# One layer of a hybrid decoder: the four output tiles in one piece, the router's work behind them

## What is computed

```python
y = jax.nn.sigmoid(gate_a) * y_a + jax.nn.sigmoid(gate_b) * y_b      # attention and LRU branch
x = _layer_norm(ALPHA * x + gate1 * (y @ w_out[l]), ln1_g[l], ln1_b[l])
u = x * (1.0 + scale2) + shift2
f = _grouped_moe(u, router_w, router_b, moe_w_gate[l], moe_w_up[l], moe_w_down[l])
x = _layer_norm(ALPHA * x + gate2 * f, ln2_g[l], ln2_b[l])
```

## Time and profile before

| what | value |
|---|---|
| runs | 768.04, 767.47, 769.25 us |
| median | 768.04 us |
| profiled execution | 767.53 us, span in the trace 765.4 us |
| TensorE matmul busy | 647.1 us (85% of the span) |
| VectorE busy | 344.2 us (45%) |
| ScalarE busy | 250.9 us (33%) |
| mean granted TensorE clock | 0.939 |
| DMA | 189.78 MB, 248 GB/s in the mean |

### The profile page before, as it was taken

The page is one execution under the profiler, slowest core; times in us unless marked ns, Lnnn a source line. Parts: engine busy times, 40 slices in busy tenths (PEclk is TensorE's granted clock), DMA queues, the critical chain, the costliest instruction groups (busy, mean ns, idle before and its releaser), DMA issues.

```text
span 765.4 us, 15490 instructions
## 1 busy us (share of the span) xinstructions
PE 647.1 (85%) x5985; PEld 424.4 (55%) x5986; DVE 344.2 (45%) x657; ACT 250.9 (33%) x522; POOL 98.2 (13%) x185
## 2 busy tenths in 40 slices
PE   0799999998989799999999339899999999999700
PEld 0275666676767577777787224455555545555400
DVE  0265444478888775585675653111111101111058
ACT  0234434557444564465401201111111111111144
POOL 0131000200000000000000032122222212222140
PEclk9999999999999899999999559999999999999955
DMA  9999767292311322213881998999999999961162
GB/s 298 373 313 308 249 220 238 105 314 79 111 44 41 99 66 82 83 56 111 296 363 74 393 419 316 421 418 418 420 419 419 418 419 420 418 261 41 48 219 110
DMA packets 83874, 189.78 MB, mean 248 GB/s; under 512 B 7384, under 2 KB 59832, under 8 KB 68480
## 3 DMA queue, kind: packets, MB, share of 16 engines
q1 hardware_dynamic: 67616, 149.05, 51.7%
q0 software_dynamic: 7376, 32.26, 11.9%
q10 hardware_dynamic: 8848, 8.01, 3.2%
HBM read 175.23 MB, written 14.07 MB: 247 GB/s over the span
## 4 chain that ended last, share of the span: by engine, by line
PE 63%; DMA 12%; DVE 12%; ACT 6%; issue 4%; SPq 2%; ACTq 0%; POOL 0%; POOLq 0%; DVEq 0%
PE psum L1485 17%; PE psum L1496 9%; DMA raw<-in_w_in_dram 7%; PE psum L1293 6%; PE psum L1295 6%; PE psum L1294 6%; DMA wu<-in_moe_w_up_dram 3%; PE psum L1414 2%; PE psum L1416 2%; PE psum L1415 2%; PE psum L1468 2%; PE psum L1259 2%; PE psum L1475 2%; SPq L398 1%; PE psum L1336 1%
## 5 line engine op out<-in xcount | busy, mean ns | idle before, releaser
L1485 PE MATMUL psum<-wg,xs 128*32 128x256 f32 x1280 | 149.8, 386 | 3.8 <-issue 2.1
L1485 PE MATMUL psum<-wu,xs 128*32 128x256 f32 x1280 | 149.2, 386 | 0.0
L1293 PE MATMUL psum<-uh,whi 128*128 128x512 f32 x336 | 137.9, 410 | 1.7 <-DVE wlo L875 1.7
L1295 PE MATMUL psum<-uh,wlo 128*128 128x512 f32 x336 | 131.3, 391 | 0.0
L1294 PE MATMUL psum<-ul,whi 128*128 128x512 f32 x336 | 131.3, 391 | 0.0
L1485 PEld LDWEIGHTS psum<-wg,xs 128*32 128x32 f32 x1280 | 73.0, 111 | 57.1 <-issue 5.5
L1192 DVE TENSOR_TENSOR h_sb<-psum,hsil 64x256 f32<-64x256 f32 x40 | 17.1, 427 | 151.8 <-ACT hsil L784 151.8
L875 DVE TENSOR_TENSOR wlo<-raw,whi 128x1024 fp32r<-128x1024 f32 x42 | 51.4, 1224 | 68.7 <-ACT whi L611 68.5
L1496 PE MATMUL psum<-wd,hT 128*32 128x256 f32 x1280 | 77.4, 382 | 0.4 <-DVE hT L1196 0.4
L1293 PEld LDWEIGHTS psum<-uh,whi 128*128 128x128 f32 x336 | 63.3, 189 | 23.4 <-issue 7.4
L1485 PEld LDWEIGHTS psum<-wu,xs 128*32 128x32 f32 x1280 | 72.0, 111 | 0.0
(11 more groups left out here) (258 smaller groups left out, 842.7 us busy)
## 6 DMA issues: line engine op xcount, KB each, us to landing
wg<-in_moe_w_gate_dram SPq DMA_DIRECT2D x32, 1024.0 KB
wu<-in_moe_w_up_dram SPq DMA_DIRECT2D x32, 1024.0 KB
wd<-in_moe_w_down_dram SPq DMA_DIRECT2D x32, 1024.0 KB
raw<-in_w_in_dram SPq DMA_DIRECT2D x42, 512.0 KB, 3.9
ada<-in_ada_w_dram POOLq DMA_DIRECT2D x16, 1024.0 KB, 5.2
ada<-in_ada_w_dram SPq DMA_DIRECT2D x8, 1024.0 KB, 17.1
y_d<-ysb ACTq DMA_DIRECT2D x160, 32.0 KB
y_d<-zrow POOLq DMA_DIRECT2D x8, 512.0 KB, 6.4
```

What stands on the lines that cost most here:

```text
L1293: mmul(bank[s % 2], h[:, k, :], uh[:, k, :], start=(k == 0), stop=False)
L1295: ins = mmul(bank[s % 2], l[:, k, :], uh[:, k, :], start=False, stop=(k == KT - 1))
L1485: ins = mmul(psum[32 * g:32 * g + 32, 0, 0:256], xs[:, k % 2, k // 2, :], wgu[slot][g // 2][:, k, (g % 2) * 256:(g % 2) * 256 + 256], star ...
```

## The change

TensorE issues the four output tiles one after the other, and only then the router's work of all four tiles. u2 gets four buffers instead of two, and VectorE's waits for the two-buffer scheme go. ScalarE's stream gets the matching order: the square roots and stores of tiles 0 to 2 first, then the copies, with the square root of tile 3 behind the copies of tile 1. SP reads the rows a2 and b2 right behind gate1, with waits for projections 40 and 41, and ahead of the x tiles. No arithmetic is changed.

```diff
-        u2 = [at(R_W + 4 * KB * i, f"u2_{i}", [P, D])[0] for i in range(2)]
+        u2 = [at(R_W + KB * o_, f"u2_{i}", [P, D])[0] for i, o_ in enumerate((0, 4, 28, 32))]
...
             sp.wait_ge(S["proj_ps"], NPROJ - 2)
             sp.dma_start(gate1r[:, :], row_of(0)).then_inc(rows_in, 16)
+            sp.dma_start(a2r[:, :], row_of(3)).then_inc(rows_in, 16)
+            sp.wait_ge(S["proj_ps"], NPROJ - 1)
+            sp.dma_start(b2r[:, :], row_of(1)).then_inc(rows_in, 16)
             sp.wait_ge(S["proj_ps"], NPROJ)
             for t in range(NT):
                 sp.dma_start(x1[:, t, :], x[0, t * P:(t + 1) * P, :]).then_inc(x1_in, 16)
-                if t == 0:
-                    sp.dma_start(a2r[:, :], row_of(3)).then_inc(rows_in, 16)
-                    sp.dma_start(b2r[:, :], row_of(1)).then_inc(rows_in, 16)
...
-            ln_sqrt(0)
-            store_u2(0)
-            ln_sqrt(1)
+            for t in range(NT - 1):
+                ln_sqrt(t)
+                store_u2(t)
             u2_columns(0)
-            store_u2(1)
             logit_parts(0)
             u2_columns(1)
-            ln_sqrt(2)
-            store_u2(2)
+            ln_sqrt(NT - 1)
             logit_parts(1)
             u2_columns(2)
-            ln_sqrt(3)
             logit_parts(2)
-            store_u2(3)
-            u2_columns(3)
-            logit_parts(3)
+            store_u2(NT - 1)
+            u2_columns(NT - 1)
+            logit_parts(NT - 1)
...
-                if t >= 2:
-                    dve.wait_ge(S["u2T_ps"], 2 * (t - 1))
-                    dve.wait_ge(u2_st[t % 2], 16 * (t // 2))
-                V.scalar_tensor_tensor(u2[t % 2][:, :].rearrange("t (k p) -> t p k", k=KT), by_k(zt), rstd[:, t:t + 1],
+                V.scalar_tensor_tensor(u2[t][:, :].rearrange("t (k p) -> t p k", k=KT), by_k(zt), rstd[:, t:t + 1],
...
-            out_tile(0)
-            out_tile(1)
-            to_router(0)
-            out_tile(2)
-            logit_parts(0)
-            to_router(1)
-            logits(0)
-            out_tile(3)
-            logit_parts(1)
-            to_router(2)
-            logits(1)
-            logit_parts(2)
-            to_router(3)
-            logits(2)
-            logit_parts(3)
-            logits(3)
+            for t in range(NT):
+                out_tile(t)
+            for t in range(NT):
+                to_router(t)
+                if t >= 1:
+                    logits(t - 1)
+                logit_parts(t)
+            logits(NT - 1)
```

More of the change, by code:

```diff
@@ L740, in store_u2 @@
                 act.wait_ge(S["u2_done"], t + 1)
-                act.dma_start(u2_d[t * P:(t + 1) * P, :], u2[t % 2][:, :]).then_inc(u2_st[t % 2], 16)
+                act.dma_start(u2_d[t * P:(t + 1) * P, :], u2[t][:, :]).then_inc(u2_st[t % 2], 16)
             def u2_columns(t):
@@ L1384, in to_router @@
                         ins = nc.tensor.transpose(psum[:, 4 + half, (k % 4) * P:(k % 4 + 1) * P],
-                                                  u2[t % 2][:, k * P:(k + 1) * P], ident)
+                                                  u2[t][:, k * P:(k + 1) * P], ident)
                     ins.then_inc(S["u2T_ps"], 1)
```

## The result

The changed kernel takes **763.65 us** in the median of 6 runs (761.84 to 764.76), the kernel before beside it 767.82 (767.37 to 769.25, 6 runs). The ratio is 0.9941, 95% interval 0.9925 to 0.9957: 3.3 to 5.8 us faster, against 5.2 to 5.4 forecast, and inside the range. The profiled execution is one of 764.76 us, the slowest of the six; its span is 762.9 (765.4 before).

A forecast was written before the change was run, and what follows sets the result against it. It took TensorE's products, VectorE's tile 3 normalisation, then TensorE's tail as the bounding chain before routing. 3.1 us from products plus 2.3 from the tail gave 5.4: 762.1 for the profiled execution, 762.6 median, range 761.0 to 767.2.

The forecast's parts named there:

- Products in one piece: TensorE's output products: interleaved router work moves behind tile 3's products, which then end 3.1 us earlier.
- VectorE and the buffers: VectorE's normalisation: same instructions; the two removed waits cost nothing before but would cost now without four buffers.
- The cover of three tiles: Router work of tiles 0 to 2, 6.9 us, hides under tile 3's 7.6 us normalisation with 0.7 to spare: cost nothing.
- ScalarE and SP: ScalarE's new order (tile 3's square root, bounds 0 to 0.3 us) and SP's earlier row reads: both taken as nothing.
- The tail: Tile 3's transposes to routing: 3.3 us at the upper clock against 5.63, 2.3 us gained; bounds 0 and 2.3.
- case A: The main forecast: products' 3.1 us and the tail's 2.3 us both gained, 762.6 us; chance 0.48.
- B: Clock lost at tile 3, around 422 to 424 us: only the products' 3.1 us stay, 764.9 us; chance 0.18.
- Behind it, nothing: Routing, gather and expert loop shift whole; the gather stays 6.2 us, so no gain or loss is added there.
- C: Clock lost inside the router block, at 418.9 us: gain of 1.2 us, 766.8 us; chance 0.15.
- E: Clock lost as soon as the products end: routing 0.7 us later, 768.7 us, or 770.3 at worst; chance 0.06.
- D: Gather ends with the third expert's weight stream, so its end moves by only 3.1 us: 764.9 us; chance 0.07.

The follow-up runs named there:

- e4: Kernel before with four u2 buffers and without VectorE's two waits, old order kept: 767.76 us, ratio 1.0006.
- e3: Changed kernel's order on all engines, but u2 in two buffers with VectorE's two waits: 767.22 us, ratio 0.9998 to the kernel before.
- e9: Changed kernel with the transposes of tiles 0 to 2 issued twice: 763.97 us, ratio 0.9955 to the kernel before.
- e10: Kernel before with only the early reads of rows a2 and b2 added: 768.02 us, ratio 1.0001.
- e12: Kernel before with five filler matmuls in TensorE's idle time ahead of tile 3's transposes, run again for its trace: 766.28 us, ratio 0.9981.
- e1: Changed kernel once more, without an edit: 763.96 us over 12 runs, ratio 0.9959 to the kernel before.
- e5: Changed kernel with one filler matmul of constants in the gap before tile 3's transposes: 763.97 us, ratio 0.9954 to the kernel before.
- e2: Changed kernel with the a2 and b2 row reads put back behind the first x tile: 761.94 us, ratio 0.9942 to the kernel before.
- e6: Changed kernel with eight unread transposes of tile 0's u2 as filler before tile 3's transposes: 762.60 us, ratio 0.9929 to the kernel before.
- e7: Changed kernel with four filler matmuls before the expert loop's first transposes: 762.97 us, ratio 0.9934 to the kernel before.
- e11: Changed kernel with row reads put back, one filler before tile 3's transposes and four before the expert loop: 762.48 us, ratio 0.9935 to the kernel before.

## Why the prediction was right, point by point

*Products in one piece, 3.1 us.* Right, 3.26 in each of the traces with the new order and four buffers. The 0.15 above the forecast 3.11 is the slower start of products after each change of work, which I left out: in the kernel before the second product behind tile 0's transposes starts 0.31 us after the first (394.54 and 394.23), where 0.23 is the rhythm, and likewise behind the logits. Nothing waited for VectorE in between.

*VectorE and the buffers.* Right: e4 shows the waits worth nothing in the old order, e3 that with two buffers and this order of ScalarE the new order wins nothing.

*The cover of three tiles.* Right and thin as said. 6.7 us of TensorE's work from 415.63 to 422.3 under 7.6 of VectorE's; 1.17 us to spare instead of 0.7: the three tiles took 6.7 us and not 6.9, mostly because tile 0 has no logits of a former tile inside it (2.13 us from 415.63 to 417.76), and VectorE began 0.2 us after the block did. e9 shows the far side.

*ScalarE and SP.* Right: the square root of tile 3 ran at 419.91 with its input at 419.88, so nothing was lost; the row reads are worth nothing (e10).

*The tail, 2.3 us.* The mechanism was right and measured twice, 2.17 in the new order and in the old one with fillers (e12). Its size in the median is the term that was put too high: it isn't there in each execution. The profiled one had 0.7 of it. I gave case A and B as alternatives for the kernel; they are alternatives for an execution.

That I took the upper bound of this term rests on one row, the stretch from 33 to 40 us that kept 1.00, and that row was luck. In the changed kernel's trace the same stretch, which the change doesn't touch, lost the clock (timeline, and a window of the same form as above):

```profile
37.84 0.63 PE L1273 MATMUL psum<-cst,x_sb 128*128 128x128 f32 x4 [2.85 <-ACT uT L632]
39.10 1.09 PE L1273 MATMUL psum<-cst,x_sb 128*128 128x128 f32 x4 [0.63 <-ACT uh L628]
...
38.00:42.00 4.00, 3.37 (x13) 2.77 (x13) 3.90 (x7) 3.49 (x6) 4.00 (x9) 0.57 1.03 424
```

It fell between 36 and 41 us in nine of the 13 traces of the table (all but before, e1, e5 and e12). So the row was no ground for 2.3 over 0, and the choice came out right in part without it.

*Behind it, nothing.* Not quite. The stretch from the first gather's issue to the loop was 8.06 to 8.17 in the five traces in which it starts after 447, and 8.12 to 8.56 in the six of the new order with four buffers and the first group unaltered (changed, e1, e2, e5, e6, e9), 0.2 more in the mean. Block 0 was 7.08 to 7.79 in the former (mean 7.39) and 7.18 to 7.84 in the latter (7.62), ranges that nearly coincide. With 3.26 and 2.17 that leaves about 5.0 us where the clock holds and 3.5 where it falls; the medians moved by 4.2 and 3.7. The 0.2 of block 0 may be the chance moment at which the clock comes back. For the 0.2 of the gather there is a sign: it took 6.18 to 6.21 us in the two traces in which the third expert's first load was issued 13.2 us ahead of it (before, e4), and 6.37 to 6.67 in the six with 10.3 to 11.1 (e1, e2, e5, e7, e9, e11), so more of that stream may lie ahead of it. Neither was tested by a run.

*The rivals.* B occurred in one trace of the four with the gap open. C and E did not occur in the changed kernel; e3 shows their price in another. D is excluded: the gather took 6.2 to 6.7 us in the traces of the new order, and in e12, where the routing ended 2.2 us earlier than before and the third expert's first load was issued only 0.9 earlier (435.36 against 436.25), it took 6.29 and its end moved along. The loop keeps what comes in: from the second group on it took 299.3 to 301.7 us in all traces, old and new.

*The rule of the Trainium skill* (TensorE: Matmul & The Clock Gate, Part 4: PE-mode transpose), that transposes don't count for the clock gate as matmuls do. The prediction drew from it that the clock falls inside the router block. Here the measurement differs, as the windows of e9 show, in which 48 transposes and the tiles' thin matmuls are followed by eight more:

```profile
414.40:420.40 6.00, 5.66 (x70) 4.58 (x68) 5.39 (x7) 2.63 (x6) 0.00 (x0) 1.00 0.62 238
420.40:427.00 6.60, 6.14 (x72) 4.97 (x68) 2.05 (x2) 3.82 (x8) 0.00 (x0) 1.00 1.02 412
```

12.6 us without one long product, all at 1.00. And in e3 the clock rose to 0.98 at 431.3 out of nothing but such a block. By that rule rival C or E would have been the usual case, 766.8 or more; in no trace of the changed kernel's order with four buffers did they occur. But the rule isn't refuted. The 56 transposes are about 6.9 of the 11.8 busy us, and no run parts their share from that of the thin matmuls. And e3 also speaks for it: there TensorE worked without a hole from 420.55 and got the upper clock back only at 431.2, after 10.7 us, while in the dense first gate and up group it came back after 3.0 us (before), 4.3 (changed) and 4.9 (e1).

## What to carry to other kernels

Work that is set into a dense stream of matmuls cost its full length here, and cost nothing behind the stream, where another engine had a longer chain to finish first: compare the two lengths, and give the data the buffers that the later reader needs, since here order and buffers were worth nothing alone. Where a term hangs on TensorE's clock, take it as a chance for each execution and not for the kernel, and expect the median to show a part of it. A stretch that kept the clock in one trace is no evidence that it keeps it: look at the same stretch in a second trace. To find a microsecond in a kernel whose runs spread over four, cut the traces into stages at common events; the medians of six runs don't resolve it.

## What the runs showed of the hardware that I had not expected

The clock can fall on little idleness: in the changed kernel it fell at about 424.4 with 1.2 idle us behind it, and in e1 it did not with the same 1.16 us. It came back in e3 during transposes and thin matmuls alone. In e11 it fell inside a dense group that had 3.07 idle us before it, and in e7 it held through the same group behind 2.92.

In the loop all traces have stalls that no semaphore explains (the profile calls them issue). They lie around the fourth and fifth block, 3.6 us in sum before (the earlier trace rows hide them in a mean), 4.3 us at once in e11 and 4.4 in e12, and the clock is at the lower level for some us after them. In e11 the wait list reads:

```profile
PE psum L1468 <- issue: 11.6, 14, 4.3
```

Their sum differs by up to 2 us between the traces (9.6 in the kernel before, 11.6 in e11, over both lines of the loop that show them); only the start of the output products differs by more. What ends them stays open.
